# Scaling token tiles on VectorE ahead of TensorE's transposes, in place of products with a diagonal matrix

## The chip, the cores and the metric

One core of a Trainium2 chip runs the whole program in one launch. The metric is device time in microseconds (us), the median of several executions. Engines: TensorE (PE in the profile; PEld are its weight loads), VectorE (DVE), ScalarE (ACT), GpSimd (POOL), and SyncE (SP), which issues the weight DMAs.

## The reference

Two transformer blocks run one after the other on a 512 x 1024 activation in float32. Every stage starts with an RMS norm over the 1024 features of each token, a gain per feature, and a product with the stage's first weights:

```
def rms_norm(x, g):
    xf = x.astype(jnp.float32)
    y = xf * lax.rsqrt(jnp.mean(xf * xf, axis=-1, keepdims=True) + EPS)
    return (y * g.astype(jnp.float32)).astype(x.dtype)

# first block
x = x + 0.5 * rms_norm(swiglu_ffn(rms_norm(x, norm_pre[0]), ffn1_in, ffn1_out), norm_post[0])
x = x + rms_norm(token_mixer(rms_norm(x, norm_pre[1]), ...), norm_post[1])
x = x + 0.5 * rms_norm(swiglu_ffn(rms_norm(x, norm_pre[2]), ffn2_in, ffn2_out), norm_post[2])
# second block
h = h + 0.5 * swiglu(rms_norm_2(h, ffn1_norm), ...)        # feed-forward
h = h + attention_mixer(rms_norm_2(h, mix_norm), ...)      # two kinds of attention, gated
h = h + 0.5 * swiglu(rms_norm_2(h, ffn2_norm), ...)        # feed-forward
h = h + sigmoid(rms_norm_2(h, ple_norm) @ w_gate) * (p @ w_proj)
```

So there are seven norms ahead of a stage, numbered here s = 0 to 6, and the first three stages also have a norm behind them.

## The kernel before

The activation x stays in SBUF as four token tiles of 128 tokens x 1024 features, with tokens on the partitions. A stage's first product wants features on the partitions, so each stage begins with an **entry** that norms and turns x. Weights stream in as chunks of 128 x 1024: SyncE loads each, and GpSimd splits it into a high and a low part (`w_hi`, L323, and `w_lo`, L325), with three buffers for each part. The activation is split in the same way (`u_hi`, `u_lo`), and each product is three matmuls, high x high, high x low and low x high (L341 to L343). In what follows these are the dense matmuls.

An entry does this for each token tile i:

1. ScalarE squares the tile and sums (L1108), then takes the root (L1110): one number for each token.
2. VectorE inverts it (L1542) and writes a 128 x 128 diagonal matrix with these numbers, identity times factor (L1544, tile `diag`).
3. TensorE computes tile^T x diagonal in eight products of 128 x 128 (`pe_turn_tile`, L381). This turns the tile and scales it at once, into PSUM. Each product takes the trace two records, so a tile has 16.

Once tiles 0 and 1 are turned (pair 0), ScalarE writes `u_hi` from PSUM with the gain (L1131), one feature block after another, and VectorE writes `u_lo` behind it (L1553). Each may be only a block or two ahead of the other. TensorE's order (`pe_enter`) is: turn tiles 0, 1 and 2, then the first weight chunk on pair 0 (24 dense matmuls 256 columns wide), turn tile 3, the second chunk on pair 0, and both chunks on pair 1. The first dense matmul waits for three blocks of `u_lo`, and each next one for its own block.

All programs are written out by hand: each engine has its own list, and semaphores hold them together. VectorE's list around an entry (`dve_out`, L1596) differs:

- s = 1, 2, 3 (the stage before has a norm behind it): for each tile, invert the root of y, multiply y from PSUM with the factor and the gain (L1578), then for the tile before L1542 and L1544, then add to x (L1590, both inputs in SBUF). Tile 3's L1544 stands in the middle of the `u_lo` blocks, behind the first four.
- s = 4, 5, 6: for each tile, add to x straight from PSUM (L1593), then L1542 and L1544, and after all four tiles the `u_lo` blocks.
- s = 0: only L1542 and L1544, as the tiles come in.

The stage's last product (L401 to L403) frees its last three weight buffers only near its end, so GpSimd splits the first chunks of the next stage during the entry.

Of the kernel before, what the change touches and what calls it, by code (L numbers as in the profile page):

```python
# [14 lines left out]
P = 128  # L15
T = 512
NT = T // P
# [25 lines left out]
C_ID, C_ONE, C_LE, C_LT, C_NSUF, C_NONE, C_NGT, C_NGE, C_LEVEL = (i * P for i in range(9))  # L43
# [81 lines left out]
class Box:  # L125


    def __init__(self, nc, a, out):
# [38 lines left out]
        sem = nc.alloc_semaphore  # L167
# [7 lines left out]
        self.post_loaded, self.y_ready, self.y_squared, self.y_root = sem("post_loaded"), sem("y_ready"), sem("y_squared"), sem("y_root")  # L175
        self.t_done, self.x_updated, self.x_squared, self.x_root = sem("t_done"), sem("x_updated"), sem("x_squared"), sem("x_root")
        self.eps_set, self.x_inv, self.y_inv = sem("eps_set"), sem("x_inv"), sem("y_inv")
        self.x_diag, self.x_turned, self.u_hi, self.u_lo = sem("x_diag"), sem("x_turned"), sem("u_hi_done"), sem("u_lo_done")
        self.norm_var, self.norm_root, self.norm_inv = sem("norm_var"), sem("norm_root"), sem("norm_inv")
        self.diag_done, self.spread_done = sem("diag_done"), sem("spread_done")  # L180

# [69 lines left out]
def x_tile(k, i):  # L251

    return k.x[:, i * D:(i + 1) * D]


def out_tile(k, i):
# [12 lines left out]
def wait_out_taken(k, eng, st, i):  # L269

    if st < 3:
        eng.wait_ge(k.t_done, NT * st + i + 1)
    else:
        eng.wait_ge(k.x_updated, NT * st + i + 1)
# [96 lines left out]

def pe_turn_tile(k, s, i):

    pe = k.nc.tensor
    pe.wait_ge(k.x_diag, NT * s + i + 1)
    if s and i in (0, 2):

        wait_out_taken(k, pe, s - 1, i + 1)
    for t in range(KD):
        c = TURN_BANK[i // 2] * T + (2 * t + i % 2) * P  # L380
        m = pe.matmul(k.psum[:, c:c + P], x_tile(k, i)[:, t * P:(t + 1) * P], k.diag[:, i * P:(i + 1) * P], start=True, stop=True)  # L381
    m.then_inc(k.x_turned, 1)


def pe_enter(k, s, name, c0=0, c1=1):

    pe_turn_tile(k, s, 0)
    pe_turn_tile(k, s, 1)
    pe_turn_tile(k, s, 2)
    pe_dense_half(k, s, name, c0, CHUNK_BANK[0], 0)  # L390
    pe_turn_tile(k, s, 3)
    pe_dense_half(k, s, name, c1, CHUNK_BANK[1], 0)
    pe_dense_half(k, s, name, c0, CHUNK_BANK[0], 1)
    pe_dense_half(k, s, name, c1, CHUNK_BANK[1], 1)
# [690 lines left out]
def act_load(k):  # L1085
    act, a = k.nc.scalar, k.a
    act.dma_start(k.const[:, 0:2 * P], a["const"][:, 0:2 * P]).then_inc(k.first_loaded, 16)
    for i in range(NT):
        act.dma_start(x_tile(k, i), a["x"][:, i * D:(i + 1) * D]).then_inc(k.x_loaded[i], 16)
    act.dma_start(k.param[:, :], a["param"]).then_inc(k.first_loaded, 16)  # L1090
    act.dma_start(k.const[:, 2 * P:], a["const"][:, 2 * P:]).then_inc(k.consts_loaded, 16)
    act.wait_ge(k.first_loaded, 32)
# [12 lines left out]
def act_square_x(k, s, i):  # L1105

    act = k.nc.scalar
    act.activation(k.junk[:, :], x_tile(k, i), ACT.Square, accum_out=k.x_ss[:, i:i + 1]).then_inc(k.x_squared, 1)  # L1108
    act.wait_ge(k.x_squared, NT * s + i + 1)
    act.activation(k.x_r[:, i:i + 1], k.x_ss[:, i:i + 1], ACT.Sqrt, bias=k.eps[0], scale=1.0 / D).then_inc(k.x_root, 1)  # L1110
# [426 lines left out]
def dve_root_x(k, s, i):  # L1537

    dve = k.nc.vector
    r = k.x_r[:, i:i + 1]  # L1540
    dve.wait_ge(k.x_root, NT * s + i + 1)
    dve.reciprocal(r, r).then_inc(k.x_inv, 1)  # L1542
    dve.wait_ge(k.x_inv, NT * s + i + 1)
    dve.tensor_scalar(k.diag[:, i * P:(i + 1) * P], k.cst(C_ID), r, None, ALU.mult).then_inc(k.x_diag, 1)  # L1544


def dve_lo(k, s, p, places=range(KD)):
# [9 lines left out]
def dve_start(k):  # L1557
    dve = k.nc.vector
    dve.memset(k.eps[0], EPS).then_inc(k.eps_set, 1)
    dve.memset(k.eps[1], 4 * EPS).then_inc(k.eps_set, 1)  # L1560
    for i in range(NT):
        dve_root_x(k, 0, i)
    dve_lo(k, 0, 0)
    dve_lo(k, 0, 1)
# [31 lines left out]
def dve_out(k, st):  # L1596
    s = st + 1
    for i in range(NT):
        if st < 3:
            dve_post(k, st, i)  # L1600
            if i:
                dve_root_x(k, s, i - 1)
            dve_update(k, st, i)
        else:
            dve_update(k, st, i)
            dve_root_x(k, s, i)
    if st < 3:
        dve_lo(k, s, 0, range(4))
        dve_root_x(k, s, NT - 1)
        dve_lo(k, s, 0, range(4, KD))  # L1610
    else:
        dve_lo(k, s, 0)
    dve_lo(k, s, 1)
# [679 lines left out]
```

## Time and profile before

| what | value |
|---|---|
| median of three runs (lowest, highest) | 2395.99 us (2393.27, 2400.38) |
| time of the profiled execution | 2393.68 us |
| its span | 2392.3 us |
| TensorE busy / VectorE / ScalarE / GpSimd | 2329.0 / 829.9 / 449.5 / 1279.4 us |
| mean granted TensorE clock | 0.986 of full |
| the 448 records of L381 on TensorE | 56.1 us busy |
| the 28 diagonals of L1544 on VectorE | 16.8 us busy |

A busy time is the sum over an engine's records. Matmuls overlap in the pipeline, so a record's duration (270 ns and more) is longer than the distance from one to the next. The profile of one execution gives the rows below; their times count from the start of the span.

### The profile page before, as it was taken

To read this page: it belongs to the slowest core of one execution; us is meant where nothing else is said; L and a number is where in the kernel's file an instruction comes from. 1 tells how busy PE (TensorE), PEld (TensorE's weight loads), DVE (VectorE), ACT (ScalarE), POOL (GpSimd) and SP (SyncE) were. 2 spreads that over 40 slices of the span, in tenths; PEclk is the share of its full clock that TensorE was granted. 3 is DMA by queue.
4 is the path that set the end of the run, shared out by engine and by line. 5 is a ranking of instruction groups with operands and counts; after the bars stand their busy time and mean duration, and the time that the engine had idled before them with its cause. 6 is when DMAs were issued, how large, how long until landed. Compare 5 with 4: busy or idle time off the path is not lost.

```text
span 2392.3 us, 26085 instructions
## 1 busy us (share of the span) xinstructions
PE 2329.0 (97%) x11060; PEld 1915.3 (80%) x11060; DVE 829.9 (35%) x872; ACT 449.5 (19%) x736; POOL 1279.4 (53%) x734
## 2 busy tenths in 40 slices
PE   7999999999999999999999999999999999999999
PEld 6888888887778888888888887877657788888887
DVE  2323104884343333005232105320578632333013
ACT  2111003323222111003111002011357121111011
POOL 4666665633255666665666665555100556666654
PEclk9999999999899999999999999999889999999999
DMA  4333332212023333332333332223000223333322
GB/s 157 97 97 97 97 97 80 80 45 62 27 87 99 97 97 97 97 97 72 97 97 97 97 97 89 79 90 98 19 1 1 71 88 97 97 97 98 105 85 83
DMA packets 55580, 201.06 MB, mean 84 GB/s; under 512 B 6408, under 2 KB 6536, under 8 KB 55336
## 3 DMA queue, kind: packets, MB, share of 16 engines
q1 hardware_dynamic: 53712, 193.62, 26.1%
q10 hardware_dynamic: 1752, 5.77, 0.6%
q8 instruction: 88, 1.44, 0.3%
q14 instruction: 28, 0.23, 0.0%
HBM read 197.27 MB, written 2.10 MB: 83 GB/s over the span
## 4 chain that ended last, share of the span: by engine, by line
PE 90%; DVE 6%; ACT 2%; issue 1%; DMA 1%; POOL 0%; ACTq 0%; DVEq 0%; POOLq 0%
PE psum L341 19%; PE psum L343 18%; PE psum L342 18%; PE psum L401 7%; PE psum L403 7%; PE psum L402 7%; PE psum L479 2%; PE psum L894 1%; PE psum L886 1%; PE psum L381 1%; ACT junk L1108 1%; DVE x L1590 1%; PE psum L923 1%; PE psum L546 1%; PE psum L439 1%
## 5 line engine op out<-in xcount | busy, mean ns | idle before, releaser
L323 POOL TENSOR_SCALAR w_hi<-w_raw 128x1024 fp32r<-128x1024 f32 (+1 forms) x365 | 388.3, 1064 | 1066.0 <-PE psum L343 657.0
L325 POOL TENSOR_TENSOR w_lo<-w_raw,w_hi 128x1024 fp32r<-128x1024 f32 (+1 forms) x365 | 891.7, 2443 | 30.5
L341 PE MATMUL psum<-u_hi,w_hi 128*128 128x512 f32 (+1 forms) x2072 | 794.8, 384 | 10.7 <-DVE work L1938 4.7
L342 PE MATMUL psum<-u_hi,w_lo 128*128 128x512 f32 (+1 forms) x2072 | 788.9, 381 | 0.0
L343 PE MATMUL psum<-u_lo,w_hi 128*128 128x512 f32 (+1 forms) x2072 | 788.7, 381 | 0.0
L341 PEld LDWEIGHTS psum<-u_hi,w_hi 128*128 128x128 f32 x2072 | 391.9, 189 | 90.3 <-issue 7.4
L343 PEld LDWEIGHTS psum<-u_lo,w_hi 128*128 128x128 f32 x2072 | 391.6, 189 | 74.4
L342 PEld LDWEIGHTS psum<-u_hi,w_lo 128*128 128x128 f32 x2072 | 391.9, 189 | 73.8 <-issue 0.7
L401 PE MATMUL psum<-w_hi,hidden_hi 128*128 128x512 f32 x800 | 311.8, 390 | 1.0 <-DVE work L1797 1.0
L402 PE MATMUL psum<-w_lo,hidden_hi 128*128 128x512 f32 x800 | 311.2, 389 | 0.0
L403 PE MATMUL psum<-w_hi,hidden_lo 128*128 128x512 f32 x768 | 298.8, 389 | 0.0
L1627 DVE TENSOR_TENSOR scratch<-scratch,psum 128x512 f32<-128x512 f32 x88 | 60.5, 688 | 586.8 <-PE psum L343 586.8
L1629 DVE TENSOR_TENSOR hidden_lo<-scratch,hidden_hi 128x512 fp32r<-128x512 f32 x88 | 239.4, 2720 | 60.8 <-ACT hidden_hi L1187 60.8
L401 PEld LDWEIGHTS psum<-w_hi,hidden_hi 128*128 128x128 f32 x800 | 150.2, 188 | 32.8 <-DVE work L1797 1.4
L402 PEld LDWEIGHTS psum<-w_lo,hidden_hi 128*128 128x128 f32 x800 | 150.2, 188 | 31.4 <-issue 0.2
L403 PEld LDWEIGHTS psum<-w_hi,hidden_lo 128*128 128x128 f32 x768 | 144.2, 188 | 29.9
L1187 ACT CAST hidden_hi<-scratch 128x512 fp32r<-128x512 f32 x88 | 55.0, 625 | 479.4 <-DVE scratch L1627 479.4
L1185 ACT ACTIVATE scratch<-psum 128x512 f32<-128x512 f32 x88 | 52.6, 598 | 345.9 <-PE psum L343 345.9
L1593 DVE SCALAR_TENSOR_TENSOR x<-psum,x 128x1024 f32<-128x1024 f32 x12 | 14.6, 1218 | 240.3 <-PE psum L403 240.3
L1572 DVE RECIPROCAL misc<-misc 128x1 f32<-128x1 f32 x12 | 1.9, 157 | 243.2 <-ACT misc L1118 243.2
L1108 ACT ACTIVATE junk<-x 128x1024 bf16<-128x1024 f32 x28 | 29.5, 1055 | 272.5 <-DVE x L1593 261.3
L381 PE MATMUL psum<-diag,x 128*128 128x128 f32 x448 | 56.1, 285 | 23.8 <-DVE diag L1544 23.8
(263 smaller groups left out, 1679.9 us busy)
## 6 DMA issues: line engine op xcount, KB each, us to landing
w_raw<-in_ffn_in SPq DMA_DIRECT2D x176, 512.0 KB, 3.5
w_raw<-in_ffn_out SPq DMA_DIRECT2D x88, 512.0 KB, 3.5
w_raw<-in_proj_in SPq DMA_DIRECT2D x34, 512.0 KB, 3.5
w_raw<-in_mix_in SPq DMA_DIRECT2D x29, 512.0 KB, 3.5
w_raw<-in_embed SPq DMA_DIRECT2D x10, 512.0 KB, 3.5
w_raw<-in_mix_out SPq DMA_DIRECT2D x8, 512.0 KB, 3.4
w_raw<-in_branch SPq DMA_DIRECT2D x8, 512.0 KB, 3.5
w_raw<-in_proj_out SPq DMA_DIRECT2D x8, 512.0 KB, 3.6
```

The costliest lines, as they stand in the source:

```text
L323: pool.tensor_scalar(hi, raw, 1.0, 1.0, ALU.mult, ALU.mult).then_inc(k.w_split, 1)
L325: pool.tensor_tensor(lo, raw, hi.bitcast(F32), ALU.subtract).then_inc(k.w_split, 1)
L341: pe.matmul(out, hi[:, cols], xhi, start=first, stop=False)
L342: pe.matmul(out, lo[:, cols], xhi, start=False, stop=False)
L343: return pe.matmul(out, hi[:, cols], xlo, start=False, stop=last)
L381: m = pe.matmul(k.psum[:, c:c + P], x_tile(k, i)[:, t * P:(t + 1) * P], k.diag[:, i * P:(i + 1) * P], start=True, stop=True)
L401: pe.matmul(bank, xhi(kk)[:, tokens], hi[:, cols], start=kk == 0, stop=False)
L402: pe.matmul(bank, xhi(kk)[:, tokens], lo[:, cols], start=False, stop=False)
L403: return pe.matmul(bank, xlo(kk)[:, tokens], hi[:, cols], start=False, stop=last)
L1187: act.copy(tile(k.hhi, i), hm).then_inc(k.hid_hi, 1)
L1627: dve.tensor_tensor(hm, sg, k.ps[CHUNK_BANK[(2 * i + 1) % 4]], ALU.mult).then_inc(k.multiplied, 1)
L1629: dve.tensor_tensor(tile(k.hlo, i), hm, tile(k.hhi, i).bitcast(F32), ALU.subtract).then_inc(k.hid_lo, 1)
```

## The change

VectorE no longer writes a diagonal. It multiplies the whole token tile, 128 x 1024, by the factors of its tokens, and writes the result to a place in the work region that holds the stage's first hidden tiles only later. TensorE then turns that copy with eight transposes against the identity. The other instructions, their order on each engine and the places of the waits are the same.

```
+def scaled_tile(k, i):
+
+    return k.big[:, (8 + 2 * i) * T:(10 + 2 * i) * T]
...
 def pe_turn_tile(k, s, i):
 
-    pe = k.nc.tensor
-    pe.wait_ge(k.x_diag, NT * s + i + 1)
+    pe, x = k.nc.tensor, scaled_tile(k, i)
+    pe.wait_ge(k.x_scaled, NT * s + i + 1)
     if s and i in (0, 2):
 
         wait_out_taken(k, pe, s - 1, i + 1)
     for t in range(KD):
         c = TURN_BANK[i // 2] * T + (2 * t + i % 2) * P
-        m = pe.matmul(k.psum[:, c:c + P], x_tile(k, i)[:, t * P:(t + 1) * P], k.diag[:, i * P:(i + 1) * P], start=True, stop=True)
+        m = pe.transpose(k.psum[:, c:c + P], x[:, t * P:(t + 1) * P], k.cst(C_ID))
     m.then_inc(k.x_turned, 1)
...
@@ dve_root_x(k, s, i)
     dve.reciprocal(r, r).then_inc(k.x_inv, 1)
     dve.wait_ge(k.x_inv, NT * s + i + 1)
-    dve.tensor_scalar(k.diag[:, i * P:(i + 1) * P], k.cst(C_ID), r, None, ALU.mult).then_inc(k.x_diag, 1)
+    dve.tensor_scalar(scaled_tile(k, i), x_tile(k, i), r, None, ALU.mult).then_inc(k.x_scaled, 1)
```

## Rows read from the trace of the kernel before

**Rows 1.** The page, part 1: busy us, share of the span, instructions

```profile
PE 2329.0 (97%) x11060; PEld 1915.3 (80%) x11060; DVE 829.9 (35%) x872; ACT 449.5 (19%) x736; POOL 1279.4 (53%) x734
```

**Rows 2.** TensorE's groups by shape: count | busy us, mean ns | idle before

```profile
L381 PE MATMUL psum<-diag,x 128*128 128x128 f32 x448 | 56.1, 285 | 23.8 <-DVE diag L1544 23.8
L472 PE MATMUL psum<-const,work 128*128 128x128 f32 x64 | 9.7, 308 | 3.9 <-DVE work L1961 2.6 <-ACT work L1218 0.8 <-ACT work L1235 0.6
```

**Rows 3.** Chain of waits, transposes and a dense matmul: start, us, what

```profile
574.92 1.94 PE psum L472 x16
...
1464.12 0.12 PE psum L343
...
1704.57 3.41 PE psum L472 x16
```

**Rows 4.** VectorE's groups by shape

```profile
L2070 DVE TENSOR_SCALAR work<-work,misc 128x512 f32<-128x512 f32 x8 | 3.9, 487 | 0.3
L2070 DVE TENSOR_SCALAR work<-work,misc 128x128 f32<-128x128 f32 x8 | 2.3, 282 | 0.0
L1988 DVE TENSOR_SCALAR work<-work 128x2048 f32<-128x2048 f32 x1 | 1.2, 1229 | 0.0
```

**Rows 5.** Timeline of the first entry: start, us, engine, line, what

```profile
17.01 0.29 DVE L1544 TENSOR_SCALAR diag<-const,misc 128x128 f32<-128x128 f32 x1
17.45 7.46 PE L381 MATMUL psum<-diag,x 128*128 128x128 f32 x48 [17.45 <-DVE diag L1544]
...
23.16 0.84 ACT L1131 ACTIVATE u_hi<-psum,param 128x256 fp32r<-128x256 f32 x2 [2.28 <-PE psum L381]
```

**Rows 6.** Chain of waits, third entry (s = 2)

```profile
707.28 1.24 DVE x L1590
...
713.42 1.71 DVE diag L1544
715.12 2.01 DVE x L1590
...
718.86 0.55 DVE diag L1544
...
721.42 0.41 DVE u_lo L1553
...
724.31 0.29 DVE diag L1544
...
727.09 1.78 PE psum L381 x16
```

**Rows 7.** Timeline of the fifth entry (s = 4), VectorE and GpSimd

```profile
1456.20 2.38 POOL L325 TENSOR_TENSOR w_lo<-w_raw,w_hi 128x1024 fp32r<-128x1024 f32 x1
...
1457.43 1.22 DVE L1544 TENSOR_SCALAR diag<-const,misc 128x128 f32<-128x128 f32 x1
...
1462.04 0.87 DVE L1553 SCALAR_TENSOR_TENSOR u_lo<-psum,param,u_hi 128x256 fp32r<-128x256 f32 x2
```

**Rows 8.** Stretches: length, busy us (records) by engine, granted clock, DMA share, GB/s

```profile
17.40:21.40 4.00, 3.95 (x19) 3.98 (x20) 1.35 (x6) 3.38 (x9) 0.00 (x0) 1.00 0.64 259
21.40:25.00 3.60, 3.51 (x32) 3.32 (x30) 1.18 (x3) 1.65 (x4) 0.00 (x0) 1.00 0.00 0
390.00:393.40 3.40, 1.27 (x12) 1.07 (x11) 3.18 (x6) 2.17 (x5) 3.40 (x2) 1.00 0.32 127
393.40:396.80 3.40, 3.10 (x16) 2.83 (x15) 2.91 (x5) 1.72 (x4) 3.32 (x2) 0.50 0.50 154
...
1489.10:1492.50 3.40, 0.00 (x0) 0.00 (x0) 3.33 (x3) 0.42 (x1) 2.58 (x2) 1.00 0.19 78
1492.50:1495.90 3.40, 3.08 (x7) 2.48 (x8) 2.06 (x4) 1.87 (x4) 0.00 (x0) 0.50 0.42 154
1704.50:1707.50 3.00, 2.93 (x14) 2.93 (x15) 2.60 (x8) 0.00 (x0) 0.00 (x0) 0.50 0.00 0
1707.50:1711.00 3.50, 1.55 (x9) 1.13 (x8) 0.00 (x0) 1.87 (x1) 0.00 (x0) 0.99 0.00 0
```

More of the change, by code:

```diff
@@ L177, in __init__ @@
         self.eps_set, self.x_inv, self.y_inv = sem("eps_set"), sem("x_inv"), sem("y_inv")
-        self.x_diag, self.x_turned, self.u_hi, self.u_lo = sem("x_diag"), sem("x_turned"), sem("u_hi_done"), sem("u_lo_done")
+        self.x_scaled, self.x_turned, self.u_hi, self.u_lo = sem("x_scaled"), sem("x_turned"), sem("u_hi_done"), sem("u_lo_done")
         self.norm_var, self.norm_root, self.norm_inv = sem("norm_var"), sem("norm_root"), sem("norm_inv")
```

## The prediction

> **What bounds the kernel now.** I read the page's busy times first. TensorE is busy for 97% of the span, and VectorE and GpSimd leave half their time or more unused [rows 1]. Taken over the whole span, a cut in TensorE's work would pay in full. So the next view is the chain of waits, in the stretches where the change acts. It shows that six of the seven entries aren't bound by TensorE. In the third entry the chain runs through VectorE and ScalarE: the diagonal of tile 1, the sum of tile 2, its squares, its diagonal, the sum of tile 3, the `u_lo` blocks, the diagonal of tile 3, and only behind these does TensorE turn tile 3 [rows 6]. The timeline of the fifth entry shows the diagonal of tile 2 at 1457.43 and the first `u_lo` at 1462.04, with dense work behind that [rows 7]. The first entry differs: there `u_hi` waits for TensorE's products [rows 5]. Last come the stretches with the granted clock [rows 8].
>
> **What TensorE saves.** Before, a tile is 16 records; 28 tiles make 448 records [rows 2]. At full clock, 16 take 1.78 us [rows 6], or 0.11 us each. The mixers' transposes (L472) have the same shape and leave one record each: 16 transposes take 1.94 us at full clock, and 3.41 us, or 0.21 each, where the clock was low [rows 3]. The first of a row starts a little late, so I take 0.11 each. Eight transposes are then 0.88 us, against 1.78: 0.9 us less for each tile, 25 us over 28. What of it shows depends on the place. Tile 3 always stands between two dense chunks, so its 0.9 us shows in every entry, if its data is there. Tiles 0 to 2 are waited for in the first entry alone.
>
> **What VectorE pays.** The diagonal takes 0.29 us where nothing holds it up [rows 5]. The new operation is eight times as wide, both sides in SBUF. The nearest rows are the softmax scalings (L2070): 282 ns for 128 columns, 487 for 512 [rows 4]. The slope is 205/384 = 0.53 ns a column, so 1024 columns take 487 + 273 = 0.76 us. The 2048 columns of L1988 in 1229 ns [rows 4] confirm it from above (interpolated: 0.73). So 0.47 us more for each tile. Both ends: 0.4 from L1988, and, if the operation ran at the pace of the plain sums (L1590, 1024 wide, 1.24 us where nothing holds it up [rows 6]), 0.95.
>
> Some diagonals took 1.71 and 1.22 us instead of 0.29 [rows 6, 7]. GpSimd's `w_lo` split ran from 1456.20 to 1458.58, and the diagonal issued at 1457.43 ended at 1458.65 [rows 7]. It waited for GpSimd and finished 0.07 us behind it. A wide operation waits just the same and then still has 896 more columns: again 0.47 us. And while it runs, GpSimd's next split waits, which moves the next collision by as much. So a stall doesn't swallow the excess, it passes it on.
>
> **Entry by entry.**
>
> - First entry (s = 0). TensorE's start moves by 0.47, from 17.45 to 17.9. The 32 records ahead of `u_hi` become 16 transposes. The pace was 0.21 us at first (19 records in 4.0 us) and 0.11 from 21.4 on [rows 8]; the first of these rows shows a clock of 1.00, but its pace is that of half the clock. All 16 transposes fall in the slow part: 15 x 0.21 = 3.2 to the start of the last, 21.1, and some 0.4 for it to drain at that pace: 21.5. `u_hi` began at 23.16 [rows 5]: 1.6 us gained. Tile 3 gives 0.9. Sum -2.5.
> - Entries s = 1, 2, 3. All four scalings are on the chain. Three are in rows 6, and tile 0's stands just ahead of tile 1's sum, which holds up GpSimd and with it tile 1's scaling. So +4 x 0.47 = +1.9, less 0.9 for tile 3: +1.0 each, +3.0 for three.
> - Entries s = 4, 5, 6. On the chain to the first `u_lo` are the scalings of tiles 0, 2 and 3 in full; that of tile 1 mostly disappears in the wait for GpSimd. +3 x 0.47 = +1.4, less 0.9: +0.5 each, +1.5 for three. TensorE's turned tiles 0 and 1 are early now, but ScalarE is at tile 3's squares until then, and VectorE's list puts tile 3's scaling ahead of `u_lo`.
>
> That is +2.0 us in sum.
>
> **The clock.** The diagonal products also kept TensorE at work. In the second entry it did 1.27 us of work from 390.0 to 393.4, and the clock was half (0.50) from 393.4 to 396.8 [rows 8]. That cost little, since it waited for `u_lo` anyway. Another fall comes behind the stretch from 1489.1 to 1492.5 without a record, and there seven 512-wide matmuls took 3.08 us [rows 8], 0.44 each. In the fifth entry the diagonal products filled the time from the stage's end at 1458 to nearly the first dense matmul at 1463.6 (tiles 0 to 2, 48 records, 5.4 us). With the change TensorE has 2.6 us of transposes there, and the first dense matmul comes 1.4 us later: some 4.5 us without work, nearly as long as ahead of 1492.5. I expect the clock to fall there, in s = 5 and 6 too, and the first dense chunk to begin at half pace. A low stretch of 3.4 us filled with dense work gives back half: 1.7 us. It can be two such stretches or part of one, so 0 to 3.4; I take 1.8 each, +5.4. In s = 1 to 3 the transposes leave still longer gaps (2.7 us of work in some 10), but the dense chunk there waits for `u_lo` half the time. I take 1.0 each, +3.0, between 0 and 3.
>
> The sum is -2.5 + 3.0 + 1.5 + 5.4 + 3.0 = +10.4 us. From the profiled execution's 2393.7 us (span 2392.3) this gives 2404.1. The median of the three runs is 2.3 us above that execution, so I give 2405.
>
> One rule speaks further against the change. Rows first: from 1704.5 to 1707.5, at half clock, TensorE ran nothing but transposes, and from 1707.5 the clock was 0.99 [rows 8]. Transposes at work ahead of a rise: they raise the clock here like other work. The Trainium skill, page "TensorE: Matmul & The Clock Gate", Part 4: PE-mode transpose, says that the full clock does not engage for transposes. This trace doesn't agree. By that rule the first entry would lose its rise at 21.4. Worked out from rows, its first dense chunk of 24 would run at 0.21 instead of 0.12 us each [rows 3, 8] (+2.2), and tile 3's eight transposes at 0.21 (+0.8). The total would be +13.4, at 2407 from the profiled execution.
>
> **The rivals.**
>
> - *The clock holds (not slower).* If TensorE's gaps aren't long enough to lower it, both clock terms vanish: +2.0, or 2395.7 from the profiled execution, about 2398 on the runs' scale. For it: from 1458 on, the fifth entry still has three tiles of transposes, and the clock was lowered in only one of the six later entries before. Against it: the gap ahead of 1492.5. It decides by how near the first dense matmul comes to tile 2's transposes: with `u_lo` no later than before, the gap would be 3 us, not 4.5.
> - *TensorE is the bound after all (faster).* If GpSimd's waits hid the wider scaling, each later entry would keep its 0.9 us and the clock would hold: -2.5 - 6 x 0.9 = -7.9, 2385.8. For it: a diagonal held up to 1458.65 was ready long before. Against it: the chain in rows 6 has each of them.
> - *VectorE at the slow pace.* With 0.95 us more in place of 0.47, the 4 + 4 + 4 + 3 + 3 + 3 = 21 scalings on chains cost 10 more: +20, 2414.
> - *The transposes don't raise the clock*: +13.4, as worked out above.
> - *The operation leaves two records per transpose* (no saving at all): refuted by rows 3, unless the new place of the data matters. It has no share.
>
> **How the numbers follow.** Less than 0.3% is no change for such a measurement, 7.2 us here. Forecast: 0.60, of which 0.12 lies below +7.2 (its terms of the clock have wide ends) and 0.48 above. Clock holds: 0.22, nearly all within 0.3%. Rule on the transposes: 0.08, slower. Slow pace: 0.05, slower. Faster case: 0.05. So faster 0.05, same 0.34, slower 0.61. The range reaches from just below the case where the clock holds (2396) to 2414, where the slow pace begins; the forecast's own range is 2400 to 2411.
>
> **What would show it.** L381's 448 records become 224 at the transposes' line; VectorE's group has 28 of 128x1024 with a shortest near 0.76 us. In the third entry, `u_lo` and tile 3's turn come 1.9 us later behind the stage's end. In the fifth, the first `u_lo` comes 1.4 us later, and the granted clock shows 0.50 within a few us of the first dense matmul. In the first, `u_hi` starts near 21.5. It is wrong if the clock stays full in the later entries, or if the gain on TensorE shows in the entries' lengths; then the second or third rival is nearer.

## The result and the profile after

| | before | changed kernel | ratio, 95% interval |
|---|---|---|---|
| median (range), 20 executions each | 2393.66 (2391.06 to 2400.38) | 2398.68 (2395.38 to 2406.6) | 1.0026 [1.0018, 1.0034] |
| profiled execution | 2393.68 | 2402.09 | |
| its span, mean granted clock | 2392.3, 0.986 | 2400.7, 0.977 | |
| a second measurement, 15 and 6 executions | 2393.21 | 2401.39 (2399.98 to 2404.41) | 1.0032 [1.002, 1.0044] |

The changed kernel is slower: by 5.0 us in the first measurement, by 8.2 in the second, by 8.4 between the profiled executions. The forecast was +10.4 on the profile's scale and 2405 as the time. The direction is right and the time lies in the range, but the first median stays under the 7.2 us that I had named as the bound of no change. The second passes it by a little. A ratio here, with its interval, comes from all executions and not from the two medians: 1.0026 is 6.2 us. One execution of the wait-free diagonal told below took 9066 us, at a clock of 1.00, and its ratio leaves it out.

The profile's first part, answering [rows 1]: TensorE lost 224 records and 11.4 us of work, and the span grew all the same. VectorE has 8.2 us more.

```profile
PE 2317.6 (97%) x10836; PEld 1901.9 (79%) x10836; DVE 838.1 (35%) x872; ACT 449.3 (19%) x736; POOL 1286.9 (54%) x734
```

TensorE's and VectorE's groups by shape (count | busy us, mean ns | idle before, and what ended it), answering [rows 2] and the diagonals of [rows 6, 7]. Of 448 records 224 are left.

```profile
L386 PE MATMUL psum<-const,work 128*128 128x128 f32 x224 | 34.4, 309 | 37.3 <-DVE work L1549 33.3 <-DVE x L1598 4.0
L1549 DVE TENSOR_SCALAR work<-x,misc 128x1024 f32<-128x1024 f32 x28 | 27.8, 994 | 1.0
```

The durations of the scaling's line (shortest, median, longest in ns, first and last start). The shortest took 0.752 us, half of them no more than 0.756; the longest ones waited.

```profile
L1549 DVE TENSOR_SCALAR work<-x,misc x28: 752/756/2174, 17.1 to 2336.2; 128x1024 f32<-128x1024 f32 x28
```

**The first entry.** The timeline (start, us, engine, line, what) answers [rows 5]. TensorE begins 0.54 us later, is done after 5.36 us instead of 7.46, and `u_hi` starts at 21.68 instead of 23.16. The entry is 2.4 us shorter.

```profile
17.09 0.75 DVE L1549 TENSOR_SCALAR work<-x,misc 128x1024 f32<-128x1024 f32 x1
...
17.99 5.36 PE L386 MATMUL psum<-const,work 128*128 128x128 f32 x24 [17.99 <-DVE work L1549]
...
21.68 0.84 ACT L1136 ACTIVATE u_hi<-psum,param 128x256 fp32r<-128x256 f32 x2 [0.71 <-PE psum L386]
```

**The third entry.** The timeline of VectorE and GpSimd answers [rows 6]. The scalings of tiles 0, 1 and 2 stand at 710.61, 714.25 and 720.13. Before, these were diagonals of 0.29, 1.71 and 0.55 us; now they take 0.76, 2.17 and 1.02, each 0.46 or 0.47 more. The waits have stayed. GpSimd's split at 713.50 ended at 715.87, and the scaling issued meanwhile ended at 716.42, 0.55 behind it; the next pair, 720.60 and 721.15, gives the same 0.55. With the diagonal that distance was 0.07 [rows 7]: the operation stood still until GpSimd was done, and then did most of its work (0.55 of 0.756 us). Compared with the same point before, `u_lo` (723.05) comes 1.35 us later. That is three scalings, and tile 3's follows behind it.

```profile
710.61 0.76 DVE L1549 TENSOR_SCALAR work<-x,misc 128x1024 f32<-128x1024 f32 x1
...
713.50 2.37 POOL L330 TENSOR_TENSOR w_lo<-w_raw,w_hi 128x1024 fp32r<-128x1024 f32 x1
...
714.25 2.17 DVE L1549 TENSOR_SCALAR work<-x,misc 128x1024 f32<-128x1024 f32 x1
...
717.41 3.19 POOL L330 TENSOR_TENSOR w_lo<-w_raw,w_hi 128x1024 fp32r<-128x1024 f32 x1
...
720.13 1.02 DVE L1549 TENSOR_SCALAR work<-x,misc 128x1024 f32<-128x1024 f32 x1
...
723.05 0.86 DVE L1558 SCALAR_TENSOR_TENSOR u_lo<-psum,param,u_hi 128x256 fp32r<-128x256 f32 x2
```

**The fifth entry.** The same view, answering [rows 7]. The first `u_lo` starts at 1466.43; seen from the stage's end it is 1.2 us later than before.

```profile
1459.69 2.38 POOL L330 TENSOR_TENSOR w_lo<-w_raw,w_hi 128x1024 fp32r<-128x1024 f32 x1
...
1461.58 1.04 DVE L1549 TENSOR_SCALAR work<-x,misc 128x1024 f32<-128x1024 f32 x1
...
1465.50 1.01 DVE L1549 TENSOR_SCALAR work<-x,misc 128x1024 f32<-128x1024 f32 x1
...
1466.43 0.86 DVE L1558 SCALAR_TENSOR_TENSOR u_lo<-psum,param,u_hi 128x256 fp32r<-128x256 f32 x2
```

**The clock.** Stretches of the third and the fifth entry (stretch, length, busy us and records of TensorE's matmuls, its weight loads, VectorE, ScalarE, GpSimd, then granted clock, DMA share, GB/s), answering [rows 8]. In the third entry TensorE had 1.09 us of work in 3.4, and the clock was 0.50 for the next 10.2 us. In the last third of those TensorE was busy throughout, with 18 records in 3.4 us; the last row has 26 in 2.8 at full clock. In the fifth it had 1.06 us of work, and 6.8 us at 0.50 follow, the first dense matmuls among them.

```profile
716.30:719.70 3.40, 1.09 (x8) 0.86 (x8) 3.36 (x4) 1.24 (x3) 3.32 (x2) 1.00 0.51 157
719.80:723.20 3.40, 1.97 (x8) 1.57 (x8) 3.23 (x4) 0.83 (x3) 3.32 (x3) 0.50 0.43 126
...
726.60:730.00 3.40, 3.40 (x18) 3.40 (x18) 1.83 (x5) 0.87 (x2) 0.00 (x0) 0.50 0.40 148
...
1463.80:1467.20 3.40, 1.06 (x8) 0.86 (x8) 1.86 (x4) 2.42 (x6) 3.40 (x2) 1.00 0.47 165
1467.30:1470.70 3.40, 2.67 (x12) 2.70 (x13) 2.63 (x6) 2.23 (x6) 2.49 (x2) 0.50 0.37 136
1470.70:1474.10 3.40, 3.40 (x18) 3.40 (x17) 0.00 (x0) 0.00 (x0) 0.00 (x0) 0.50 0.49 154
1474.20:1477.00 2.80, 2.80 (x26) 2.80 (x25) 1.55 (x4) 1.86 (x5) 0.00 (x0) 1.00 0.00 0
```

Before, one of the six later entries had such a stretch, of 3.4 us. Now all six have: 10.2 us in each of s = 1, 2 and 3, then 6.8, 3.4 and 6.8.

**The entries as a table.** For each entry I took from both traces the time from the last product of the stage ahead to three points behind it, and the difference between the kernels, in us:

| later than before (us) | s=0 | 1 | 2 | 3 | 4 | 5 | 6 | sum |
|---|---|---|---|---|---|---|---|---|
| first dense matmul | -1.5 | 1.35 | 1.35 | 1.34 | 1.18 | 1.19 | 1.19 | |
| tile 3's turn | -1.5 | 2.03 | 2.66 | 1.97 | 3.48 | 2.56 | 3.62 | |
| end of the entry | -2.4 | 1.11 | 1.79 | 1.06 | 2.99 | 1.65 | 2.78 | +9.0 |

The entries hold 9.0 us; the code between them, which is the same in both kernels, came out 0.6 us shorter, and 9.0 - 0.6 is the 8.4 between the spans. That 0.6 is small by luck: the mixer behind the second entry took 1.6 us more, the attention mixer behind the fifth 2.2 less. In the other eleven profiles these two stretches of unchanged code came out between 0.1 less and 4.7 more, and between 2.2 and 8.2 less, than in the profile of before. So a profile's entries compare the edits better than its span or a median does. The first line is the same within 0.02 us in the entries of each kind: it is VectorE's delay alone. What varies comes in behind it, where the clock acts.

### The profile page after: what moved, and what is told of

It reads as the page before. It is cut to its first block, busy times and chain, and to the rows that moved or that the text cites. A ratio compares the mean times of both kernels' runs of the same rounds, so it can differ in the third digit from the quotient of the medians.

```text
span 2400.7 us, 25637 instructions
## 1 busy us (share of the span) xinstructions
PE 2317.6 (97%) x10836; PEld 1901.9 (79%) x10836; DVE 838.1 (35%) x872; ACT 449.3 (19%) x736; POOL 1286.9 (54%) x734
## 4 chain that ended last, share of the span: by engine, by line
PE 90%; DVE 7%; ACT 2%; issue 1%; DMA 1%; ACTq 0%; DVEq 0%
PE psum L346 19%; PE psum L347 19%; PE psum L348 19%; PE psum L408 7%; PE psum L406 7%; PE psum L407 7%; PE psum L484 1%; ACT junk L1113 1%; DVE work L1549 1%; PE psum L899 1%; PE psum L891 1%; DVE x L1595 1%; PE psum L928 1%; PE psum L551 1%; PE psum L1037 1%
## 5 line engine op out<-in xcount | busy, mean ns | idle before, releaser
L328 POOL TENSOR_SCALAR w_hi<-w_raw 128x1024 fp32r<-128x1024 f32 (+1 forms) x365 | 395.8, 1084 | 1067.0 <-PE psum L348 657.1
L347 PEld LDWEIGHTS psum<-u_hi,w_lo 128*128 128x128 f32 x2072 | 396.9, 192 | 73.9 <-issue 0.7
L386 PE MATMUL psum<-const,work 128*128 128x128 f32 x224 | 34.4, 309 | 37.3 <-DVE work L1549 33.3
```

Of the source, the lines that this page charges most:

```text
L328: pool.tensor_scalar(hi, raw, 1.0, 1.0, ALU.mult, ALU.mult).then_inc(k.w_split, 1)
L347: pe.matmul(out, lo[:, cols], xhi, start=False, stop=False)
```

## The experiments

Each is told with the difference of its median against the kernel before on the same chip, and with the sum of its seven entries against the profile of before, taken like the table above. The median is of all executions, the entries are of one. The edits are to the changed kernel unless told otherwise.

**Product with the scaled tile.** VectorE's part is as changed; TensorE does a full product with the identity, two records each, in place of the transpose. What it tells apart: how much is VectorE's, and how much TensorE's.

```diff
-        m = pe.transpose(k.psum[:, c:c + P], x[:, t * P:(t + 1) * P], k.cst(C_ID))
+        m = pe.matmul(k.psum[:, c:c + P], x[:, t * P:(t + 1) * P], k.cst(C_ID), start=True, stop=True)
```

> The changed kernel with TensorE turning the scaled tile by a plain product with the identity (two records for each of the eight, 1.78 us for a tile) in place of a transpose. VectorE's work is that of the change, TensorE's that of the kernel before. My theory (two costs: the wider scaling on VectorE's chain, and the lower clock behind TensorE's shorter work): the clock is kept in the fifth to seventh entries, but nothing is saved on TensorE. Against the kernel before: first entry +0.5 us (its start), second to fourth +1.8 each, fifth to seventh +1.2 each, in all +9 to +10, though no clock is lost in the last three. The rival that the clock is the whole loss expects 0 to +1 us here. The rival that VectorE's excess hides in its waits for GpSimd expects about +0.5 us.

Measured: 2404.93 against 2394.06, +10.9 us, ratio 1.0046 [1.0033, 1.0059]; entries +11.5. That the two agree is luck: the profiled execution is the fastest of five, its span is 5.3 us longer than before, and its attention mixer took 8.0 less. The first entry ends 0.96 us later, where 0.5 was expected. The entries s = 1, 2 and 3 each end 1.81 us later, which is four scalings at 0.47 less 0.07, and s = 4, 5, 6 have the first dense matmul 1.18 to 1.20 later. Its stretches of the fifth and sixth entry (columns as above):

```profile
1465.50:1469.00 3.50, 3.50 (x33) 3.46 (x32) 2.35 (x3) 1.02 (x4) 3.42 (x3) 1.00 0.25 55
1469.00:1472.40 3.40, 2.12 (x19) 1.92 (x18) 1.98 (x5) 2.42 (x7) 3.35 (x2) 1.00 0.42 117
...
1473.30:1476.70 3.40, 3.40 (x19) 3.40 (x18) 1.76 (x4) 1.34 (x4) 1.51 (x1) 0.50 0.33 113
...
1968.30:1971.50 3.20, 3.20 (x27) 3.20 (x28) 1.97 (x5) 1.59 (x4) 1.78 (x1) 1.00 0.42 120
```

Where the changed kernel had 1.06 us of work ahead of the dense chunk, this one has 2.12. Of s = 4 to 6 only one had a low stretch (3.4 us), and that entry ended 2.67 later; s = 1 and 2 had one each, mostly ahead of the first dense matmul, which cost nothing. Of the late ones, the two without ended 1.19 and 1.24 later. So scaling costs 1.8 in the middle entries and 1.2 in the late ones, and a low stretch of 3.4 us over dense work costs some 1.5.

**Transposes alone.** TensorE transposes the tile as it is, and VectorE makes the diagonal as before: the norm factors are left out of the computation. It is the change without VectorE's price.

```diff
-    pe, x = k.nc.tensor, scaled_tile(k, i)
+    pe, x = k.nc.tensor, x_tile(k, i)
...
-    dve.tensor_scalar(scaled_tile(k, i), x_tile(k, i), r, None, ALU.mult).then_inc(k.x_scaled, 1)
+    dve.tensor_scalar(k.diag[:, i * P:(i + 1) * P], k.cst(C_ID), r, None, ALU.mult).then_inc(k.x_scaled, 1)
```

> TensorE transposes the token tiles as they are, and VectorE writes the small diagonal as before, which nobody reads (the norm factors are left out). TensorE's side of the change alone. My theory: first entry -2.9 us; second to fourth -0.9 each and perhaps +0.3 for the clock; fifth to seventh -0.9 each, the first dense matmul no later than before, and part of a low stretch each (0 to +1.7), since TensorE then stands idle for some 2.8 us ahead of it. In all -5 us, between -8 and -2. The rival that the clock is the whole of the change's loss expects at least +3 us against the kernel before; the rival that VectorE's excess alone is the loss expects -8.

Measured: 2387.72 against 2394.06, -6.3 us, 0.9981 [0.9972, 0.999]; but its profiled execution has a span of 2391.8, and its entries sum to -0.1: -2.7 in the first, then -0.6, +0.9, +0.5, +0.6, +0.6 and +0.7. The first dense matmul comes when it came before, in every entry. So 0.9 of saving for tile 3 has become a loss in five of six entries, and nothing but the clock is there to do it. The profiled execution is one of the slowest three of eleven; the other eight took 2386 to 2388 us, and what their entries lost was not seen. The stretches are of the fifth entry:

```profile
1460.40:1463.80 3.40, 0.77 (x7) 0.56 (x6) 2.40 (x6) 2.70 (x9) 3.32 (x3) 1.00 0.56 159
1464.90:1468.30 3.40, 3.40 (x18) 3.40 (x18) 0.88 (x2) 0.38 (x1) 0.44 (x1) 0.50 0.50 146
```

18 dense records in 3.4 us where the kept-busy kernel below has 29 at full clock: this is the stretch that costs 1.5.

**Kept busy.** The changed kernel with products that nobody reads: tile 1 turned three times, and 6 or 12 products of the identity behind tile 2's turn. Neither delays anything that is waited for.

```diff
-    for t in range(KD):
+    for t in list(range(KD)) * (3 if s and i == 1 else 1):
...
+    if s:
+        c = TURN_BANK[1] * T + P
+        for _ in range(12 if s > 3 else 6):
+            k.nc.tensor.matmul(k.psum[:, c:c + P], k.cst(C_ID), k.cst(C_ID), start=True, stop=True)
```

> The changed kernel with work of no use for TensorE where it would stand idle, in entries two to seven: tile 1 is transposed three times in place of once (the same values again), and behind tile 2 stand 6 products of 128 x 128 into columns that tile 3 overwrites later, 12 in the fifth to seventh entries (2.7 us). My theory: the clock is full again when the first dense chunk of the fifth to seventh entries begins, and these entries are +0.3 us each against the kernel before (+1.2 for the scaling, -0.9 for tile 3's transposes) in place of +1.7 to +3.0 in the changed kernel's profile; second to fourth +0.9 each, with a low stretch still possible; first -2.4. In all +1 us against the kernel before, 4 us faster than the changed kernel. If the clock is not what costs, it is as slow as the changed kernel or slower.

Measured: 2393.3 against 2394.06, -0.8 us, 1.0002 [0.9992, 1.0011]; entries +2.8, the first at -2.36. With added work the change's 5 to 8 us are gone from the median. The entries s = 1 to 3 end at +0.91, +0.93 and +0.90, and s = 4 and 5 at +0.29 and +0.30: as 1.81 - 0.9 and 1.2 - 0.9 give. Stretches of the fifth and of the seventh entry:

```profile
1462.90:1466.30 3.40, 3.40 (x33) 3.40 (x32) 1.99 (x4) 2.39 (x7) 3.40 (x2) 1.00 0.42 128
1467.00:1470.40 3.40, 3.40 (x29) 3.40 (x30) 2.05 (x5) 1.67 (x4) 1.85 (x1) 1.00 0.38 124
...
2334.00:2337.40 3.40, 3.40 (x8) 2.73 (x9) 1.75 (x4) 1.32 (x4) 1.49 (x1) 0.50 0.36 98
```

The fourth still had a low stretch of 3.4 us, nearly all of it ahead of its first dense matmul, and lost nothing by it. The seventh fell too, and was the one entry that came out late, at +1.87. These three experiments show the clock's part: the same transposes and scalings cost 6.2 us less in the entries (2.8 in place of 9.0) when TensorE has something to do in the wait. By the medians it is 5.8 against the first measurement of the changed kernel and 9.0 against the second.

**Scaling twice.** A second scaling of each tile, into a place nobody reads, ahead of the first.

```diff
+    dve.tensor_scalar(k.big[:, (KF + 8 + 2 * i) * T:(KF + 10 + 2 * i) * T], x_tile(k, i), r, None, ALU.mult)
```

> The changed kernel with each wide scaling done twice, the first time into a place that nobody reads: 0.76 us more of VectorE for each tile. My theory says that four of these stand on the chain in the second to fourth entries, three in the fifth to seventh and one in the first: 22 x 0.76 = +16.7 us against the changed kernel, about +22 against the one before. The rival that VectorE's excess hides where it waits for GpSimd (tiles 1 and 2) expects 2 in each later entry: +9 to +10 us against the changed kernel.

Measured: 2426.35 against 2394.06, +32.3 us, 1.014 [1.0127, 1.0154]; entries +38.1, with the clock low for 10.2 to 13.7 us in each of the six later ones. Against the changed kernel that is some 27 us, and all theories had expected less. Nothing of it hides, which goes against the rival by which GpSimd's waits swallow it. But my price of 0.76 for each operation on the chain was too small as well: the first dense matmul is 4.1 us later than in the changed kernel in s = 1 to 3 and 5.8 in s = 4 to 6, where three operations ahead of it, as I had them, make 2.3. The timeline of its fifth entry, VectorE and GpSimd, shows why:

```profile
1471.42 1.05 POOL L328 TENSOR_SCALAR w_hi<-w_raw 128x1024 fp32r<-128x1024 f32 x1 [10.07 <-PE psum L408]
1471.75 1.26 DVE L1549 TENSOR_SCALAR work<-x,misc 128x1024 f32<-128x1024 f32 x1
1472.55 2.69 POOL L330 TENSOR_TENSOR w_lo<-w_raw,w_hi 128x1024 fp32r<-128x1024 f32 x1
1472.93 2.86 DVE L1550 TENSOR_SCALAR work<-x,misc 128x1024 f32<-128x1024 f32 x1
```

The added scaling (L1549) waits for one operation of GpSimd (to 1472.47) and ends 0.54 behind it; GpSimd meanwhile starts its next split, and the second scaling waits for that one too, until 1475.24. Two of these in a row take turns with GpSimd, here at 1.3 and 2.9 us, not 0.76 each. Only because the change has one operation for one was my +0.47 right.

**Transposes only where TensorE is waited for.** The first entry and tile 3 keep the change; the other 18 tiles go back to the product with the diagonal. By the steps above it should keep every gain and leave out each loss.

```diff
+        if s == 0 or i == 3:
             m = pe.transpose(k.psum[:, c:c + P], x[:, t * P:(t + 1) * P], k.cst(C_ID))
+        else:
+            m = pe.matmul(k.psum[:, c:c + P], x_tile(k, i)[:, t * P:(t + 1) * P], k.diag[:, i * P:(i + 1) * P], start=True, stop=True)
...
-    dve.tensor_scalar(scaled_tile(k, i), x_tile(k, i), r, None, ALU.mult).then_inc(k.x_scaled, 1)
+    if s == 0 or i == 3:
+        dve.tensor_scalar(scaled_tile(k, i), x_tile(k, i), r, None, ALU.mult).then_inc(k.x_scaled, 1)
+    else:
+        dve.tensor_scalar(k.diag[:, i * P:(i + 1) * P], k.cst(C_ID), r, None, ALU.mult).then_inc(k.x_scaled, 1)
```

> Scaling and transposes as in the change for all tiles of the first entry and for tile 3 of the six later ones; tiles 0 to 2 of those by the diagonal and the products, as before. My theory: the first entry -2.4 us as in the changed kernel; each later one -0.9 for tile 3's transposes and +0.47 for its wider scaling, and the clock as in the kernel before, since TensorE's products stay. In all -2.4 - 6 x 0.43 = -5 us against the kernel before, between -3 and -6. The rival that a wide scaling costs more than its own length wherever GpSimd works expects 0 to -2.

Measured: 2383.63 against 2394.39, -10.8 us, 0.9952 [0.994, 0.9964]. Its entries sum to -5.0: -2.3 in the first and -0.44 to -0.47 in each of the six others (0.9 saved by TensorE, 0.47 paid by VectorE for tile 3). VectorE's groups by shape (count | busy us, mean ns | idle before):

```profile
L1555 DVE TENSOR_SCALAR diag<-const,misc 128x128 f32<-128x128 f32 x18 | 13.0, 724 | 0.6
L1553 DVE TENSOR_SCALAR work<-x,misc 128x1024 f32<-128x1024 f32 x10 | 8.4, 840 | 0.3
```

No entry has a low stretch. Two stretches of the fifth, with 2.28 us of TensorE's work where the changed kernel had 1.06, and 29 records at full clock behind it:

```profile
1458.80:1462.20 3.40, 2.28 (x22) 2.12 (x20) 2.58 (x6) 2.27 (x8) 3.32 (x3) 1.00 0.51 148
1462.20:1465.60 3.40, 3.40 (x29) 3.40 (x30) 2.04 (x5) 1.66 (x4) 1.85 (x1) 1.00 0.49 129
```

**The same once more**, unaltered, in another set of runs.

> e5_transposes_where_hidden once more: its entries gave -5.0 us together, but its median -10.8, and some 6 us of that lay in the attention mixer, which is the same code in all kernels, at a place where the clock was low in the profile of the kernel before and not here. If that is chance, the median of these runs is nearer to -5 against the kernel before (-4 to -8) or the runs spread between the two; if the shorter entries lead to it, they repeat -10 to -11 and the mixer's low stretch is missing again.

Measured: 2383.53 against 2393.21, -9.7 us, 0.9972 [0.9957, 0.9987], which is -6.7 us over all executions, as two of the nine took 2393 and 2395; entries -5.0, and one low stretch of 3.4 us, in the second entry, which cost nothing. It beats both kernels in both sets, and the entries give the same -5.0 twice. The medians have 5 to 6 us more than the entries, and those lie in code that is the same in all kernels. In the profile of before, the attention mixer behind the fifth entry has the clock at 0.50 from 1857.7 on for 10.2 us, in this one it stays full at that place. Stretches of before, then of this kernel:

```profile
1857.70:1861.10 3.40, 2.63 (x10) 1.93 (x9) 2.45 (x6) 0.00 (x0) 0.68 (x1) 0.51 0.00 0
...
1864.50:1867.90 3.40, 3.40 (x11) 2.19 (x11) 1.40 (x1) 0.00 (x0) 2.78 (x2) 0.50 0.45 154
```

```profile
1850.30:1853.70 3.40, 2.31 (x16) 1.81 (x15) 3.36 (x8) 0.00 (x0) 0.99 (x1) 1.00 0.00 0
...
1857.10:1860.50 3.40, 3.40 (x24) 2.59 (x22) 1.11 (x3) 0.00 (x0) 2.47 (x2) 1.00 0.49 154
```

11 records against 24 in 3.4 us. That mixer took 6.4 to 6.6 us less here than in the profile of before. Shorter entries are not needed for that: the product with the scaled tile (-8.0) and the scaling done twice (-6.7) have it too, with longer entries. Nor does the kernel alone decide it: the one that has both gains, below, has it at -8.2 in one profile and -2.2 in the next. But times as low as these aren't equally frequent: 12 of this kernel's 14 took at most 2388 us, and one of the 37 of the kernel before in the same two sets did. Why stays open, so of the 10 to 11 us by which its medians are lower only the entries' 5.0 are explained.

**A diagonal that doesn't wait.** The kernel before, with another form of the same operation for the diagonal: it also leaves a sum over the row, which nobody reads.

```diff
-    dve.tensor_scalar(k.diag[:, i * P:(i + 1) * P], k.cst(C_ID), r, None, ALU.mult).then_inc(k.x_diag, 1)
+    dve.tensor_scalar(k.diag[:, i * P:(i + 1) * P], k.cst(C_ID), r, 0.0, ALU.mult, ALU.add, accum_out=k.misc[:, 248 + i:249 + i]).then_inc(k.x_diag, 1)
```

> The kernel before, with the diagonal written by the form of the same operation that also writes out its sum (into a column that nobody reads). If VectorE's diagonals wait for GpSimd because their form takes a resource that both share, and the form with the sum doesn't take it, then the diagonals of 1.7 and 1.2 us are down to some 0.3 to 0.4 plus the sum's read-out. The sums of x behind them (two inputs in SBUF) then wait themselves, but stand first in line when GpSimd ends its split: second to fourth entry -0.7 us each, fifth to seventh -0.4 each, -3 us in all against the kernel before. The rival that VectorE waits for something else in those places (ScalarE's root, a semaphore) expects the same long diagonals and 0 us.

Measured: 2390.18 against 2394.39, -4.2 us, 0.998 [0.9963, 0.9997]; entries -3.1 (the profiled execution has a span 9.5 us under that of before), of which -0.74 each in s = 1 to 3 and -0.3 each in s = 4 to 6. Its group by shape (count | busy us, mean ns | idle before); 28 records that read the sum out, of 0.08 us each, come beside it:

```profile
L1544 DVE TENSOR_SCALAR_CACHE_REDUCE diag<-const,misc 128x128 f32<-128x128 f32 x28 | 9.7, 346 | 1.0
```

The timeline of its third entry, VectorE and GpSimd:

```profile
711.94 2.37 POOL L325 TENSOR_TENSOR w_lo<-w_raw,w_hi 128x1024 fp32r<-128x1024 f32 x1
712.69 0.34 DVE L1544 TENSOR_SCALAR_CACHE_REDUCE diag<-const,misc 128x128 f32<-128x128 f32 x1
712.96 2.42 DVE L1590 TENSOR_TENSOR x<-x,scratch_f 128x1024 f32<-128x1024 f32 x1
714.27 2.02 POOL L323 TENSOR_SCALAR w_hi<-w_raw 128x1024 fp32r<-128x1024 f32 x1
```

The diagonal that took 1.71 us [rows 6] takes 0.34 in the midst of GpSimd's split. Of these 1.37 us 0.74 reach the end of the entry. Part of the wait has moved: the sum behind it takes 2.42 where it took 2.01 [rows 6], and GpSimd's own next operation is stretched to 2.02 us (1.05 at that place in the kernel before, from 715.01 on). I did not follow the rest.

**Scaling in the form that doesn't wait.** The same form for the changed kernel's wide scaling.

```diff
-    dve.tensor_scalar(scaled_tile(k, i), x_tile(k, i), r, None, ALU.mult).then_inc(k.x_scaled, 1)
+    dve.tensor_scalar(scaled_tile(k, i), x_tile(k, i), r, 0.0, ALU.mult, ALU.add, accum_out=k.misc[:, 248 + i:249 + i]).then_inc(k.x_scaled, 1)
```

> The changed kernel with all 28 wide scalings in the form that also writes out its sum. At one result per cycle I expect some 1.2 us for each in place of 0.76, but no wait for GpSimd: tile 1's in the second to fourth entries (2.2 us in the changed kernel's trace) gains 0.9, those of tiles 0 and 3 lose 0.5 each. In all 0 to +6 us against the changed kernel. If GpSimd's port is what makes e4_scaling_twice cost 26 us over the changed kernel, no scaling here is longer than 1.4 us; a rival in which VectorE's wide operations wait for anything else keeps some at 2 us.

Measured: 2400.4 against 2394.39, +6.0 us, 1.0028 [1.0018, 1.0038]; entries +13.7. The durations of its line:

```profile
L1549 DVE TENSOR_SCALAR_CACHE_REDUCE work<-x,misc x28: 1278/1279/1280, 17.2 to 2338.3; 128x1024 f32<-128x1024 f32 x28
```

All 28 within 2 ns: no wait is left, but the form needs 0.52 us more than the free scaling's 0.756. The first dense matmul comes 0.5 us later than in the kernel before in s = 1 to 3, where the changed kernel had 1.35, and 2.8 later in s = 4 to 6, where it had 1.2. The clock was low in all six later entries, for 6.8 to 10.2 us. Against the changed kernel that is 4.7 us more in the entries, while the medians lie 1 us above its first difference and 2 below its second: it is no way to rescue the change. It also fits that the changed scaling's long ones were waits and not work.

**Both that gained.** Transposes where TensorE is waited for, and for the other 18 tiles the diagonal that doesn't wait.

```diff
     else:
-        dve.tensor_scalar(k.diag[:, i * P:(i + 1) * P], k.cst(C_ID), r, None, ALU.mult).then_inc(k.x_scaled, 1)
+        dve.tensor_scalar(k.diag[:, i * P:(i + 1) * P], k.cst(C_ID), r, 0.0, ALU.mult, ALU.add, accum_out=k.misc[:, 248 + i:249 + i]).then_inc(k.x_scaled, 1)
```

> e5_transposes_where_hidden and e6_diagonal_one_port together: the form with the sum for the diagonals that are left (tiles 0 to 2 of the later entries). My theory: the two add up, -5 - 3 = -8 us against the kernel before, and this version beats both kernels. If the waits for GpSimd only move to the next operation, it is no faster than e5_transposes_where_hidden.

Measured: 2383.64 against 2394.39, -10.8 us, 0.9964 [0.9952, 0.9975]; entries -6.8 (-2.5, three times -0.98, -0.47, -0.47, -0.44).

> e7_both once more, beside e10_hidden_again on the same chip: the entries gave -6.8 us for it and -5.0 for the other, its runs lay between 2380 and 2393 us. I expect it 1.8 us faster than e10_hidden_again in the entries of the profile, and faster than the kernel before by 5 to 10 us in the median; the difference between the two medians may be less than the runs' spread.

The same kernel again: 2385.09 against 2393.21, -8.1 us, 0.9967 [0.9954, 0.9979]; entries -6.7. The entries are 1.8 and 1.7 us better than with the transposes for 10 tiles and the plain diagonal; the medians (2383.6 and 2385.1 against 2383.6 and 2383.5) don't show it. The wait-free diagonal is worth 0.5 us in each of s = 1 to 3 and nothing in s = 4 to 6, and that is less than the rest of the kernel varies.

**The changed kernel again**, unaltered, beside the last two.

> The changed kernel unaltered, once more. If the clock's falls in the later entries are a matter of how the low stretches happen to lie against the entries, the scaling's share is the same as in its first profile (first dense matmul 1.35 us later in the second to fourth entries, 1.18 in the fifth to seventh) and only the rest, the clock's share, differs: 0.2 to 1 us in each of the second to fourth, 1 to 3 in each of the fifth to seventh. Clock low in all six of them. In all +4 to +8 us against the kernel before. If the clock's share were fixed by the program, all six entries would repeat to 0.1 us.

Measured: 2401.39 against 2393.21, +8.2 us, 1.0032 [1.002, 1.0044]; entries +9.8, with low stretches in all six later entries, of the same lengths as in the first profile. The first dense matmul is later by 1.32 to 1.34 and 1.18 to 1.19, as in the first. Five of the six entries end within 0.2 us of where they did. The second (s = 1) ends at +2.12 in place of +1.11: its 10.2 low us lie 2.3 later against the first dense matmul, at 395.13 there and 395.17 here, and so cover more of the dense work. That is over the 1 us that I had given as the clock's most in these entries, and in the fourth it took less than the 0.2 that I had as its least. The first row is of the first profile, the others are of this one:

```profile
399.00:402.00 3.00, 3.00 (x28) 3.00 (x28) 0.69 (x3) 0.94 (x3) 0.00 (x0) 1.00 0.02 5
```

```profile
397.90:401.20 3.30, 3.30 (x17) 3.30 (x17) 1.05 (x3) 0.68 (x2) 0.00 (x0) 0.50 0.28 109
401.30:404.30 3.00, 3.00 (x28) 3.00 (x27) 1.70 (x4) 2.02 (x5) 0.00 (x0) 1.00 0.00 0
```

## Why the prediction was right, and where its sizes were off

| step, us | predicted | entries of the profile |
|---|---|---|
| first entry | -2.5 | -2.4 |
| s = 1, 2, 3: scaling less tile 3's gain | +3.0 | +2.7 |
| s = 4, 5, 6: the same | +1.5 | +0.9 |
| clock, s = 4, 5, 6 | +5.4 | +6.5 |
| clock, s = 1, 2, 3 | +3.0 | +1.3 |
| sum | +10.4 | +9.0 |

The second and third lines are measured without the clock in them: the kept-busy kernel ended its undisturbed entries at +0.9 and +0.3. The clock's lines are what is left of the table of entries. That the sum came within 1.4 us is partly luck: the clock cost 1.1 more than predicted in the late entries and 1.7 less in the middle ones.

- *TensorE saves 0.9 a tile, and it shows only for tile 3 and in the first entry.* Right. Transposes only there gave -5.0 twice, which is -2.3 - 6 x 0.46, the 0.46 being what tile 3's scaling leaves of 0.9.
- *Scaling takes 0.76, so 0.47 more, and a wait passes it on.* Right: 0.756 measured, and 0.46 or 0.47 more on each operation in the third entry, waits included.
- *Four scalings are on the chain in s = 1 to 3.* Right, 1.81 in the kernel with full products. I had said that `u_lo` comes 1.9 later; it came 1.35, three scalings, since the fourth lies behind it.
- *Three in s = 4 to 6, that of tile 1 lost in the wait.* The size is near, 1.2 against 1.4, but the tiles were others. Seen from the stage's end, tile 2's scaling in the fifth entry (1461.58) starts 0.94 later than its diagonal (1457.43): those of tiles 0 and 1 show in full. Tile 2's took 1.04 where the diagonal took 1.22, as it was issued later in GpSimd's split and waited less. Tile 3's took 1.01 where the diagonal took 0.59 (the row below, of the kernel before). 0.94 - 0.18 + 0.42 is 1.18. So a wait can swallow part of the excess after all, against what I had written, when earlier delays move the operation inside it.

```profile
1461.53 0.59 DVE L1544 TENSOR_SCALAR diag<-const,misc 128x128 f32<-128x128 f32 x1
```

- *The clock falls in all later entries.* Right; the mechanism that decided the sign is this one. Without it the change is worth next to nothing: -0.8 in the median of the kept-busy kernel, +1.2 by the first three lines of this table. "The clock holds" was the nearest rival and failed on the row from 1467.3 to 1470.7. "TensorE is the bound" failed on the first dense matmul, later in all six. "Slow pace" failed on 0.756.
- *The transposes don't raise the clock.* It failed in the first entry, by the stretches of the changed kernel. Up to 23.4 only transposes were at work, 16 records in 3.25 us, and in the stretch from 23.4 on, the first dense matmuls included, 25 records took 3.0 us, or 0.12 each. The column of the clock reads 1.00 in both rows; the pace tells that it rose behind the transposes. In the kernel with the transposes alone it rose in the midst of them: the stretch up to 21.0 has 16 records in 3.3 us and the one from 21.1 on has 10 in 1.1, and TensorE had run nothing but transposes. So the rule of the Trainium skill ("TensorE: Matmul & The Clock Gate", Part 4: PE-mode transpose), that the full clock does not engage for them, did not hold for these fp32 transposes. The first two rows are of the changed kernel, the others of the transposes alone:

```profile
20.10:23.40 3.30, 3.25 (x16) 2.85 (x14) 2.46 (x6) 2.36 (x7) 0.00 (x0) 1.00 0.00 0
23.40:26.80 3.40, 3.00 (x25) 3.03 (x26) 2.45 (x6) 1.91 (x5) 0.00 (x0) 1.00 0.00 0
```

```profile
17.70:21.00 3.30, 3.25 (x16) 3.28 (x17) 0.90 (x4) 3.20 (x9) 0.00 (x0) 1.00 0.72 290
21.10:22.20 1.10, 1.08 (x10) 0.84 (x8) 0.80 (x3) 0.93 (x3) 0.00 (x0) 1.00 0.00 0
```

**The mis-sized term is the clock.** In s = 1 to 3 I took +1.0 each and found 0.2, 0.9 and 0.2. The low stretches were there, 10.2 us each, but most of them lay over waits and over a dense chunk that waits for `u_lo` anyway. And I gave the clock one value for all executions, where it has several. The 20 executions of the changed kernel fall into two groups: ten have a mean granted clock of 0.980 and spans of 2394.1 to 2396.4, ten have 0.976 to 0.978 and spans of 2398.3 to 2405.3. The profiled one (0.977, 2400.7) is of the second group, and so the entries' +9.0 describes that one; the first median lies between the groups. From 0.980 to 0.977 is 0.003 x 2400 = 7 us of lost full clock, or 14 us more at half, and the groups are some 6 us apart. The second set of six had only 0.976 to 0.979, hence +8.2. In which stage the first group keeps its clock is open: none of them was profiled. It need not be an entry, since the attention mixer alone, unchanged code, differs by as much as 6 us between profiles.

So the forecast was right in sign and mechanism, 6 us too high against the first median and 4 against the second.

## What to carry to other kernels

A waiting engine's cheaper instruction isn't a gain: use it where that engine is waited for (here 10 of 28 tiles), and keep the version that is cheap for the engine on the chain everywhere else. When work is taken out of TensorE's waits, look at what the granted clock does to the dense matmuls behind them, since here that cost 7.8 us in the profiled execution, nearly as much as the wider VectorE operations in the same entries (3 x 1.8 + 3 x 1.2 = 9.0). With medians that differ by less than the clock's scatter, compare the traces stage by stage: the first dense matmul of each of the six later entries repeated within 0.03 us between two traces of the changed kernel, whose medians stood 3 us apart in their difference to the kernel before.

## What the runs showed of the hardware that I had not expected

- In the scaling done twice, operations of VectorE that waited for GpSimd did so one by one: a second one right behind the first waited for GpSimd's next split, 2.86 us for 0.756 of work.
- The same multiplication with a sum over the row beside it isn't held up by GpSimd: 345 to 349 ns for 128 columns and 1278 to 1280 for 1024, whatever GpSimd did, and 0.08 us more to read the sum out. Free of waits, the plain form takes 0.29 us and 0.756.
- The time of one and the same kernel goes roughly with the mean granted clock of the execution. Of the kernel before, in one set of 15, the fastest execution (span 2384.1) had 0.990, the slowest (2394.6) 0.986; those at 0.988 had 2387.0 to 2392.8. An unchanged stretch, the attention mixer, differed by up to 8 us between profiles, as much as the change itself.
